# Two-block transformer layer on one core: scores of two key tiles on two halves of TensorE's rows, values of two heads side by side, weights in eight buffers, a few buffers and table loads moved

## The reference, cut to what matters

```
x = x + [gated delta rule | multiscale pool] @ w_out            # first block, mixer
x = x + peer(rmsnorm(x))       # per token 8 heads x 16 experts out of 16384, rows gathered from HBM
x = rmsnorm(x)
# second block: stick-breaking attention, then a SwiGLU feed-forward
q, k, v = split(h @ w_qkv)                                      # 16 heads of 64
z    = q k^T / 8
mask = s_pos < t_pos
sp   = where(mask, softplus(z), 0)
rest = reverse cumulative sum of sp over the keys
a    = exp(where(mask, z - rest, -inf));   o = a v
x = x + gate * rmsnorm(o @ w_o);   x = x + gate * rmsnorm((silu(h w_g) * (h w_u)) @ w_ffn_out)
```

## Time and profile before

| | us |
|---|---|
| median of 3 runs | 2421.37 |
| profiled execution | 2417.53 |
| its span | 2415.7 |
| TensorE busy | 1834.4 (76%) |
| VectorE busy | 1284.1 (53%) |
| ScalarE busy | 869.8 (36%) |
| GpSimd busy | 899.9 (37%) |
| mean granted TensorE clock | 0.831 |

### The profile page before, as it was taken

How to read it: one execution, slowest core, us unless ns; L and a number is a source line. 1 busy time by engine, 2 the same in 40 slices (tenths; PEclk the granted TensorE clock), 3 DMA queues, 4 the chain that set the end, 5 groups by cost and what they waited for, 6 DMA issues and landing times. The chain is left out here.

```text
span 2415.7 us, 25198 instructions
## 1 busy us (share of the span) xinstructions
PE 1834.4 (76%) x8848; PEld 1127.5 (47%) x8848; DVE 1284.1 (53%) x2785; ACT 869.8 (36%) x2323; POOL 899.9 (37%) x699
## 2 busy tenths in 40 slices
PE   8897898777778787563433468884478996999997
PEld 7764666455435264110100023320065675888786
DVE  5522668786686666556767665555403523333201
ACT  3122344334344333243633353333315634222122
POOL 1300334365563443344455544445300011444343
PEclk9999888777688889686555589995589998999999
DMA  6112999999899999999999999999751011222121
GB/s 252 42 61 69 404 406 403 407 390 404 342 379 418 418 418 417 418 414 403 420 420 419 392 373 418 419 418 419 316 174 45 1 70 39 101 105 105 70 105 52
DMA packets 106766, 685.15 MB, mean 284 GB/s; under 512 B 12048, under 2 KB 12048, under 8 KB 38416
## 3 DMA queue, kind: packets, MB, share of 16 engines
q0 software_dynamic: 73728, 536.90, 54.2%
q1 hardware_dynamic: 32912, 146.64, 16.2%
HBM read 681.40 MB, written 2.10 MB: 283 GB/s over the span
## 5 line engine op out<-in xcount | busy, mean ns | idle before, releaser
L710 PE MATMUL ps<-arena 128*32 128x512 f32 (+5 forms) x4376 | 889.1, 589 | 370.5 <-ACT arena L1363 343.9
L1601 POOL DMA_INDIRECT arena<-in_experts,arena_u x512 | 601.4, 1175 | 797.0 <-PE ps L710 704.3
L1906 DVE CUSTOM_DVE_ANT_0 arena<-arena 128x1024 f32<-128x1024 f32 x512 | 648.1, 1271 | 398.0 <-DMA arena<-in_experts,arena_u 381.8
L710 PEld LDWEIGHTS ps<-arena 128*128 128x128 f32 (+2 forms) x4376 | 449.1, 168 | 736.4 <-ACT arena L1363 512.2
L1622 POOL TENSOR_TENSOR r_low<-middle,r_low 128x1024 fp32r<-128x1024 f32 x74 | 177.9, 2405 | 492.0 <-ACT r_low L1444 492.0
L1359 ACT ACTIVATE sel<-sel 128x1 f32<-128x1 f32 x512 | 102.7, 201 | 694.5 <-DVE sel L1906 687.7
L710 PE MATMUL ps<-r_low 128*128 128x512 f32 x1248 | 285.4, 390 | 6.3 <-DVE r_low L1963 4.9
L710 PEld LDWEIGHTS ps<-r_low 128*128 128x128 f32 x1248 | 233.5, 188 | 57.7 <-DVE r_low L1963 5.6
L710 PE MATMUL ps<-upper,arena 128*128 128x384 f32 (+5 forms) x640 | 165.8, 416 | 8.6 <-DMA arena<-in_w_qkv 3.8
L1363 ACT ACTIVATE arena<-arena,sel 128x32 f32<-128x32 f32 x512 | 164.5, 321 | 16.9 <-ACT sel L1359 0.2
L1444 ACT ACTIVATE r_low<-middle 128x1024 fp32r<-128x1024 f32 x74 | 78.2, 1058 | 216.3 <-PE ps L710 216.3
(11 more groups left out here) (202 smaller groups left out, 1714.0 us busy)
## 6 DMA issues: line engine op xcount, KB each, us to landing
arena<-in_w_front SPq DMA_DIRECT2D x88, 512.0 KB, 3.7
middle<-in_w_late SPq DMA_DIRECT2D x18, 2048.0 KB, 8.1
arena<-in_w_qkv SPq DMA_DIRECT2D x48, 512.0 KB
gtrow<-in_w_ada SPq DMA_DIRECT2D x32, 512.0 KB
arena<-in_experts,arena_u POOLq DMA_INDIRECT x512
arena<-in_w_ada SPq DMA_DIRECT2D x16, 512.0 KB, 8.4
x<-in_x SPq DMA_DIRECT2D x4, 512.0 KB, 8.6
arena<-in_sub_keys SPq DMA_DIRECT2D x2, 1024.0 KB, 10.5
```

The costliest lines, as they stand in the source:

```text
L710: return nc.tensor.matmul(out_, lhsT, rhs, start=start, stop=stop_, skip_group_check=skip)
L1601: nc.gpsimd.indirect_dma_start(ring[n % RING], None, a["experts"], bass.IndirectOffsetOnAxis(ap=idxq[:, i % 4, k:k + 1], axis=0),).then_in ...
L1906: nc.vector.tensor_tensor_reduce(r[:, 0:D], r[:, 0:D], xrep[k % 4], 1.0, 0.0, ALU.mult, ALU.add, dots[:, n % 8:n % 8 + 1]).then_inc(s["dot ...
```

## The change

1. `bank_xr`: in `xr0` (token tile 0) the 8 steps write banks 5, 6, 7 in turn; step k waits for the copy of step k - 3. Later tiles stay with bank 5.
2. Group 1 of the `qkv` weights goes into the eight 4 KB buffers `wide` (0 to 32 KB), which are ring buffers 0 to 3 of the gather. The first eight units wait for `slot_done` of the last loads in these buffers, the others for the unit eight before.
3. After unit 15 SyncE's queue copies q with its two 64-partition halves exchanged (8 DMAs of 64 partitions, SBUF to SBUF, 2 MB in all), after unit 23 the first key tile of k (4 DMAs, 0.5 MB). It waits first for ScalarE's copies of the last q tile, and of the last k tile.
4. Scores: tile b = 1 goes first, then b = 0 from the exchanged copies, on the other 64 partitions, then b = 2 and 3. All wait for the second exponential of h - 2.
5. Values: in every odd step from step 3 on, two heads together, their matmuls alternating, one on output partitions 0 to 63, the other on 64 to 127. Probabilities are in four buffers.
6. ScalarE loads the activation tables at given places (`preload_act_table_set`), and the last `split` before the norm (`UNIT_FIN + 1`) stands behind it. `tail_sq2` lies elsewhere.

```diff
+        def bank_xr(t, k):
+            return 5 + k % 3 if t == 0 else 5
+        def qkv_slot(g, j):
+            if g == 0:
+                return unit_slot(2 * FRONT + j)
+            n = j % WIDE
+            return n, -(-(QUERY0 - n) // WIDE) + j // WIDE + 1
+        q_at = [80, 82, 104, 106, 162, 164, 166, 138]
+        k_at = [109 + i / 2 for i in range(6)] + [96.5, 97]
+            for j in range(QKV2):
+                n, _ = qkv_slot(1, j)
+                if j < WIDE:
+                    sp.wait_ge(s["slot_done"], LOADS - RING + j // 2 + 1)
+                else:
+                    sp.wait_ge(s["used"], 2 * FRONT + QKV2 + j + 1 - WIDE)
+                sp.dma_start(unit_buf[n], a["w_qkv"][j]).then_inc(w_unit[n], 16)
+                if j == 15:
+                    sp.wait_ge(s["qkv"], qkv_out(1, KD - 1))
+                    for lo, n in ((0, 2), (2, 2), (4, 3), (7, 1)):
+                        for half in (0, 64):
+                            sp.dma_start(region3(q_at[lo], n, S)[half:half + 64, :, :], q2[64 - half:128 - half, lo:lo + n, :]).then_inc(s["qswap"], 16)
+                if j == 23:
...
-                        if h >= 2 and b < 2:
-                            pe.wait_ge(s["at"], 2 * (h - 2) + b + 1)
+                    if h >= 2:
+                        pe.wait_ge(s["at"], 2 * (h - 2) + 2)
+                    for b in (1, 0, 2, 3):
+                        if b == 0:
+                            mm(zcols(h, b), k_swap[h // 2][other, :], q_swap[h // 2][other, :], True, False, True)
+                        else:
+                            mm(zcols(h, b), kT2[own, h // 2, b * P:(b + 1) * P], q2[own, h // 2, b * P:S], b != 3, False, True)
...
+                if step % 2 == 1 and step >= 3:
+                    i = (step - 3) // 2
+                    pe.wait_ge(s["at"], 4 * i + 4)
                     for b in range(T):
+                        for e in range(2):
+                            h = 2 * i + e
+                            ins = mm(ps[64 * e:64 * e + 64, 6 + i % 2, b * P:S], v2[b][:, h * 64:(h + 1) * 64],
+                                     spb[h % 4][:, ZAT[b]:ZAT[b] + S - b * P], b == 0, b == T - 1, True)
...
             out_pair(sc, AH // 2 - 1)
-            for u in range(UNIT_O2 + 2, UNIT_FIN + 2):
+            nc.scalar.preload_act_table_set("sqrt_and_others")
+            for u in range(UNIT_O2 + 2, UNIT_FIN + 1):
                 split(u)
...
                 if t >= 1:
                     stats_after(t - 1)
+            nc.scalar.preload_act_table_set("silu_and_others")
+            split(UNIT_FIN + 1)
...
+            nc.scalar.preload_act_table_set("sqrt_and_others")
             for u in range(UNIT_FOUT + 2, UNITS):
```

More of the change, by code:

```diff
@@ L542, in block_kernel @@
         v2 = [region(kb, D) for kb in (140, 168, 128, 100)]
+        q_at = [80, 82, 104, 106, 162, 164, 166, 138]
+        k_at = [109 + i / 2 for i in range(6)] + [96.5, 97]
+        q_swap = [region(kb, S) for kb in q_at]
+        k_swap = [region(kb, P) for kb in k_at]
         y_hT = upper3(144, KD, S)
         ZW = 1280
-        spb = [upper3(144 + 5 * n, 1, ZW)[:, 0, :] for n in range(3)]
+        spb = [upper3(144 + 5 * n, 1, ZW)[:, 0, :] for n in range(3)] + [upper3(132, 1, ZW)[:, 0, :]]
         sp_hi, sp_lo = high3(84, 1, ZW)[:, 0, :], high3(89, 1, ZW)[:, 0, :]
@@ L664, in _ @@
             sp.dma_start(prow_fin, a["prow"][1:2, :].broadcast_to([P, D])).then_inc(s["pfin"], 16)
-            for j in range(2 * QKV2):
-                n, _ = unit_slot(2 * FRONT + j)
+            for j in range(QKV2):
+                n, _ = qkv_slot(0, j)
                 if j >= NARROW:
                     sp.wait_ge(s["used"], 2 * FRONT + j + 1 - NARROW)
-                sp.dma_start(unit_buf[n], a["w_qkv"][j % QKV2]).then_inc(w_unit[n], 16)
+                sp.dma_start(unit_buf[n], a["w_qkv"][j]).then_inc(w_unit[n], 16)
+            for j in range(QKV2):
+                n, _ = qkv_slot(1, j)
[3 more added lines that the diff above has]
+                    sp.wait_ge(s["used"], 2 * FRONT + QKV2 + j + 1 - WIDE)
+                sp.dma_start(unit_buf[n], a["w_qkv"][j]).then_inc(w_unit[n], 16)
+                if j == 15:
[4 more added lines that the diff above has]
+                if j == 23:
+                    sp.wait_ge(s["qkv"], qkv_out(1, 2 * KD - 1))
+                    for lo, n in ((0, 6), (6, 2)):
+                        for half in (0, 64):
+                            sp.dma_start(region3(k_at[lo], n, P)[half:half + 64, :, :], kT2[64 - half:128 - half, lo:lo + n, 0:P]).then_inc(s["kswap"], 16)
             for m in range(LATE):
@@ L1135, in _ @@
                 if h < AH:
-                    for b in range(T):
-                        if h >= 2 and b < 2:
-                            pe.wait_ge(s["at"], 2 * (h - 2) + b + 1)
-                        mm(zcols(h, b), kT2[h % 2 * 64:h % 2 * 64 + 64, h // 2, b * P:(b + 1) * P], q2[h % 2 * 64:h % 2 * 64 + 64, h // 2, b * P:S], b != 3, False, True)
+                    own, other = slice(h % 2 * 64, h % 2 * 64 + 64), slice(64 - h % 2 * 64, 128 - h % 2 * 64)
+                    if h == 0:
+                        pe.wait_ge(s["qswap"], 16 * 8)
+                        pe.wait_ge(s["kswap"], 16 * 4)
+                    if h >= 2:
[5 more added lines that the diff above has]
+                            mm(zcols(h, b), kT2[own, h // 2, b * P:(b + 1) * P], q2[own, h // 2, b * P:S], b != 3, False, True)
                     if h == 0:
@@ L1462, in _ @@
                     sc.wait_ge(s["z"], h + 1)
-                    if h >= 3:
-                        sc.wait_ge(s["av"], h - 2)
+                    if h >= 4:
+                        sc.wait_ge(s["av"], h // 2 - 1)
                     zz = psf[:, h % 2 * 1536:h % 2 * 1536 + ZW]
-                    nc.scalar.activation(spb[h % 3], zz, ACT.Abs).then_inc(s["lnp"], 1)
+                    nc.scalar.activation(spb[h % 4], zz, ACT.Abs).then_inc(s["lnp"], 1)
                     sc.wait_ge(s["lnp"], 3 * h + 1)
-                    nc.scalar.activation(spb[h % 3], spb[h % 3], ACT.Exp, scale=-1.0).then_inc(s["lnp"], 1)
+                    nc.scalar.activation(spb[h % 4], spb[h % 4], ACT.Exp, scale=-1.0).then_inc(s["lnp"], 1)
                     sc.wait_ge(s["lnp"], 3 * h + 2)
-                    nc.scalar.activation(spb[h % 3], spb[h % 3], ACT.Ln, bias=1.0).then_inc(s["lnp"], 1)
+                    nc.scalar.activation(spb[h % 4], spb[h % 4], ACT.Ln, bias=1.0).then_inc(s["lnp"], 1)
                 if step == AH // 2:
@@ L1477, in _ @@
                         sc.wait_ge(s["rest"], 2 * h + n + 1)
-                        nc.scalar.activation(spb[h % 3][:, lo:hi], psf[:, h % 2 * 1536 + lo:h % 2 * 1536 + hi], ACT.Exp).then_inc(s["at"], 1)
+                        nc.scalar.activation(spb[h % 4][:, lo:hi], psf[:, h % 2 * 1536 + lo:h % 2 * 1536 + hi], ACT.Exp).then_inc(s["at"], 1)
                     if h % 2 == 0 and h >= 2:
@@ L1931, in _ @@
                 ve.wait_ge(s["lnp"], 3 * h + 3)
-                stt(spb[h % 3], zz, 0.0, spb[h % 3], ALU.max, ALU.add).then_inc(s["spd"], 1)
+                stt(spb[h % 4], zz, 0.0, spb[h % 4], ALU.max, ALU.add).then_inc(s["spd"], 1)
                 ve.wait_ge(s["spd"], h + 1)
```

38 lines of the change are left out of this document (18 added, 20 removed).

## The result

The changed kernel takes 2404.57 us (median of 15 runs, 2397.7 to 2418.53), the kernel before, beside it, 2422.14 (15 runs, 2414.61 to 2429.98): 0.9934 of it [0.9919, 0.9949] (in brackets, here and below: the 95% interval), 17.6 us less. The forecast was 2391, some 30 less. It is faster, clear of the 0.3% that can be told apart, by six tenths of what I said. The time lies outside the forecast's own range (2384 to 2399) and inside the wide one (2381 to 2407).

A forecast was written before the change was run, and what follows sets the result against it. The gather was taken as DMA bound, so its start and end matter, with TensorE busy throughout attention. Terms summed to -28.6 from 2417.5, so 2389, 2392.5 as median; forecast 2391, own range 2384 to 2399, wide 2381 to 2407.

The forecast's parts named there:

- `xr0`: Front, token tile 0 in three banks: steps without the copy wait, -6.6 us, bounds 0 and -7.
- First weights: Gather's end: three units no longer compete, -3.7 us; eight issued late share the engines, +3.2; value -0.5.
- Group 1: `qkv` group 1 with eight buffers: no stalls for weights, scores start at 1809.9 for 1817.76, -7.8 us.
- 8 issues of some 0.35 us each: SyncE's queue behind unit 15: the copies make unit 16 late by 3 to 4 us, with 10 still left.
- Scores: Attention: score matmuls on different row halves run beside each other, 1.55 us a head for 2.46.
- first rival: Attention scores stay serial: 17.4 us a pair, attention +6 for -6, kernel 2403; chance 0.14.
- Values: Attention: two heads' values side by side take the 2.30 us of one head, saving 2.30 a pair.
- What attention gets of that: Attention: steps of 7.45 (ScalarE bound) and 8.34 us, together 15.8 a pair for 16.56, -6 in all.
- fourth rival: TensorE's clock falls in attention's idle time: at 1.2 GHz 10.7 us more a pair, +86, 2477; chance 0.05.
- Nothing less than -13 is to be had: Attention: claimed limit of the gain while ScalarE's queue stands as it is (wait halved: 6.6 + 7.4).
- Norm and end: Norm behind the output product, `split` moved and table loaded early: -6.4 us; kernel's end without a table load: -1.3.
- All three signs: Prediction wrong if attention does not shrink, the gather ends later by its own start, or attention's clock is under 0.9.

The follow-up runs named there:

- e8: Changed kernel with token tile 0's `xr0` rows through one PSUM bank again: 2412.61 us, 0.9969 of the kernel before.
- e7: Changed kernel with group 1's weights through three buffers again instead of eight: 2422.79 us, a single run.
- e5: Changed kernel with all scores serial again and 14 filler matmuls in TensorE's wait of the even attention steps: 2409.46 us, 0.9957 of the kernel before.
- e1: Changed kernel with 14 small unused matmuls in TensorE's wait of the even attention steps: 2394.33 us, 0.9895 of the kernel before.
- c3: Changed kernel, no filler matmuls; first group 1 units after the whole gather, q copies spread behind units 17 to 20, values in two parts, two `split`s moved: 2396.39 us.
- c4: As c3, but with filler matmuls in the even attention steps and the q copies behind unit 15 as in the change: 2383.00 us, 0.9823.
- e6: Changed kernel with the last `split` ahead of the norm again, table preloads kept: 2415.09 us, a single run.

## Why the prediction was right, and where not

**`xr0`**: right in size (-6.7), in what is last next (TensorE's own queue), and in reaching the end (e8).

**First weights**: sharing with the gather as assumed, +3.7 at its end for +3.2. The -3.7 for the units that no longer compete is not seen by itself: to load 500 the 13 executions with the change average 1472.3, 3 less than the one of before, with a range of 10.6, and e7, which loads three units inside the gather again, has 1473.39. The working of the +3.2 does not come out: a third of the bytes for 7 us at the 419 GB/s of the earlier trace rows is 1.0 MB and not 1.3, so +2.4. That the forecast is near is in part luck.

**Group 1**: -6.9 for -7.8. The step "8 issues of some 0.35 us each" failed: they took 7.83 us, and the load behind them landed 8.2 us later; eight buffers covered all but 2.24 us of it. The -6.9 is one execution; over the eight kernels with the change's group 1 it is -4.4 to -8.4.

**Scores**: 1.49 for 1.55, so the first rival is out; its pair of 17.4 was measured as 17.23 in e5. The Trainium skill's page "TensorE: Matmul & The Clock Gate", section "Why this matters for your kernels", had matmuls of few rows in row groups of their own running concurrently; the trace agrees, with 6 ns between the starts of the first two records (1844.433 and 1844.439).

**Values**: side by side as taken from the earlier trace rows, 2.30 a pair at the full clock.

**What attention gets of that**: the step that failed. "Together 15.8 for 16.56" is right at the clock of the earlier trace rows (15.52 in e1). Even so e1's stage is 139.24, which is -4.4 and not -6: the first step takes 0.5 us more than before, and the pair of steps with the two `split`s 1.4 more where the others take 1.0 less. But the sum took that clock for granted while it took a quarter of TensorE's work away (12.4 for 16.56). What it got is 17.07 a pair. I had this as the fourth rival, at 5 in 100, priced at 10.7 a pair with the low clock throughout, and in proportion for a part. It came as 3.4 us of low clock in 17, for 1.55 a pair and 10 in all: enough to turn the sign of the stage, not that of the kernel. "Against: group 1 of `qkv` has gaps as long, with 0.96 granted" was a bad comparison: that stage of the kernel before has one gap of 2.07 us and else gaps of 0.41 to 0.78, attention now has 2.33 and 0.90 in every pair. The other argument, that a slow array fills its own gaps, is borne out: TensorE is busy for 3.40 of the 3.40 us. That this brings the clock back is not shown. The Trainium skill's page "TensorE: Matmul & The Clock Gate", section "A second HAM failure mode: psum-queue depth-cycling", says that short idle stretches between groups of matmuls can make the clock alternate; the trace agrees, at 2.33 us in after, though in c3 the clock stayed up behind two such waits. I had not weighed it.

"Nothing less than -13 is to be had" of attention was wrong too: its own 6.6 + 7.4 is 14.0 a pair, -20 in all, and c4 has 128.74, which is -14.9, though with the `split`s moved.

**Norm and end**: -6.5 and -1.3, as worked out; e6 gives the share of the `split` (5.9).

With the measured terms the sum is -6.7 + 1.2 - 6.9 + 5.7 - 6.5 - 1.3 = -14.5, for -28.6. Of the missing 14.1 attention is 11.7, and of that the clock 10.1 (149.32 for e1's 139.24).

All three signs that I had named for the prediction being wrong came: attention did not shrink, the gather ended later by its own start (1503.9 us from the first gather to the product of load 511, for 1502.6; less than it scatters), and the clock in attention was 0.87. That the median still lies between 2381 and 2407 is luck: the wide range had been drawn for other causes, and that 2404.57 is near the 2403 of the first rival, which was not what happened, is chance.

## What to carry to other kernels

When a change takes work from a TensorE that was busy without a break, and another engine then sets the pace, price the waits with the clock: here 2.33 us of waiting cost 1.55 us a pair more (in c3 not every such wait did), and 1.6 us a pair of matmuls with no use gave ten us back. An edit that is right by itself (two heads' values at the price of one) can lose until the other edits let its gain through, so measure it both alone and with the clock kept. Copies within the on-chip memory cost the queue that issues them as well as the transfer (7.83 us for eight): put them where nothing urgent is behind them.

## What the runs showed of the hardware

- Two float32 matmuls of 64 rows, on different row halves and into different PSUM banks, run side by side: 1280 columns in 1.49 us for 2.46.
- Issues on SyncE's queue took 0.33 to 0.60 us for a weight load of 512 KB, 0.55 to 1.38 for the copies of q within the on-chip memory and 0.65 to 3.54 for those of k (after, 1779 to 1801 us). Why the copies take longer was not tested.
- Behind waits of the same length TensorE's clock fell once and stayed up once: in c3 the steps behind waits of 2.36 and 2.35 us were granted 0.68 and 1.00.
- Before the changed code is reached, executions of nearly the same program differ by up to 5.7 us (start of `xr0`, 215.9 to 221.6 with the change, 214.27 before). The profiles of before and after, one execution each, differ by half of what the medians do.
